# One transformer layer on one core: the MLP up projection by seven half-size products

## The reference

```
x = x + g1 * (mix_lat @ w_out)                       # attention part, before
h = modulate(x, g_mlp, sh2, sc2)                     # 1024 tokens x 1024
x = x + g2 * (square(relu(h @ w_mlp1)) @ w_mlp2)     # 1024 -> 4096 -> 1024
```

## Time and profile before

| what | value |
|---|---|
| runs | 1396.66, 1398.19, 1398.62 us |
| profiled execution: span, first to last instruction | 1394.5 us |
| profiled execution: its own time | not given apart from the span |
| mean granted TensorE clock | 0.994 |
| end of the last projection, start of the MLP's units | about 730 us |
| last stretch (down projection of chunk 7) starts | 1347.7 us |
| HBM read, written | 108.4 MB, 31.7 MB |

### The profile page before, as it was taken

One profiled execution on the slowest core, in us unless ns is written; L12 is line 12 of the kernel. 1 busy time (PEld: TensorE's weight loads), 2 busy tenths in 40 slices (PEclk: granted clock), 3 DMA queues, 4 the chain that ended last, 5 costly groups with the idle time before them and its releaser, 6 DMA issues.

```text
span 1394.5 us, 18825 instructions
## 1 busy us (share of the span) xinstructions
PE 1351.0 (97%) x7262; PEld 1144.5 (82%) x7262; DVE 914.7 (66%) x1284; ACT 692.6 (50%) x1343; POOL 487.0 (35%) x321
## 2 busy tenths in 40 slices
...
GB/s 376 189 172 161 173 159 290 125 90 86 128 197 141 183 131 192 71 1 61 37 71 121 32 30 91 31 76 31 69 40 27 91 31 76 31 64 44 15 61 121
DMA packets 121576, 143.42 MB, mean 103 GB/s; under 512 B 8184, under 2 KB 103288, under 8 KB 118672
## 3 DMA queue, kind: packets, MB, share of 16 engines
...
q0 software_dynamic: 256, 0.05, 0.0%
...
## 4 chain that ended last, share of the span: by engine, by line
PE 77%; DVE 12%; ACT 6%; DMA 2%; issue 1%; POOL 1%; SPq 0%; DVEq 0%; ACTq 0%
PE f_ps L2065 24%; PE f_ps L2334 19%; PE a_ps L1425 7%; PE o_ps L1773 6%; PE a_ps L1441 5%; PE a_ps L1471 5%; PE f_ps L2350 3%; ACT s_pr L1522 3%; DVE s_nmx L1607 2%; PE t_ps L956 2%; DMA t_wm<-in_w_mod 1%; PE t_ps L945 1%; PE t_ps L971 1%; ACT l_pr L1539 1%; DVE l_nb L1612 1%
## 5 line engine op out<-in xcount | busy, mean ns | idle before, releaser
L2065 PE MATMUL f_ps<-h,f_w 128*128 128x512 f32 x1536 | 358.0, 389 | 0.4 <-DVE h L1839 0.3
L2065 PEld LDWEIGHTS f_ps<-h,f_w 128*128 128x128 f32 x1536 | 288.2, 188 | 60.6 <-DVE h L1839 0.7
L2264 DVE TENSOR_TENSOR mix<-mix,f_ps 128x512 f32<-128x512 f32 x196 | 128.8, 684 | 152.8 <-PE f_ps L2334 152.8
L2105 POOL TENSOR_TENSOR f_w<-f_w,f_g 128x1024 f32<-128x1024 f32 x30 | 77.1, 2592 | 389.9 <-DMA f_w<-in_w_mlp 342.5
L2142 ACT ACTIVATE f_a<-f_ps 128x512 f32<-128x512 f32 x64 | 38.2, 597 | 255.0 <-PE f_ps L2065 254.9
L2334 PE MATMUL f_ps<-f_bl,f_ah 128*128 128x512 f32 x392 | 152.6, 389 | 0.0
L2334 PE MATMUL f_ps<-f_bh,f_ah 128*128 128x512 f32 x392 | 152.6, 389 | 0.0
L2334 PE MATMUL f_ps<-f_bh,f_al 128*128 128x512 f32 x392 | 152.5, 389 | 0.0
L1621 DVE TENSOR_TENSOR l_pT<-a_ps,l_pT 128x512 fp32r<-128x512 f32 (+1 forms) x192 | 109.0, 594 | 53.0 <-ACT l_pT L1532 53.0
L1425 PE MATMUL a_ps<-l_k,l_q 96*128 96x512 f32 (+1 forms) x576 | 136.4, 366 | 0.5 <-DVE l_mo L1633 0.5
L956 PE MATMUL t_ps<-w_in,t_h 128*128 128x416 f32 (+2 forms) x600 | 123.4, 351 | 0.3 <-DVE w_in L719 0.3
...
## 6 DMA issues: line engine op xcount, KB each, us to landing
...
f_w1r<-in_w_mlp SPq DMA_DIRECT2D x32, 512.0 KB, 4.1
f_w<-in_w_mlp SPq DMA_DIRECT2D x16, 1024.0 KB, 5.0
t_wm<-in_w_mod SPq DMA_DIRECT2D x8, 1024.0 KB, 12.6
...
```

The costliest lines, as they stand in the source:

```text
L2065: last = nc.tensor.matmul(ps[:, b, :], w1[:, g % 2, w, k, :], h2[x][:, k, half * HB:(half + 1) * HB], start=(k == 0 and i == 0), stop=(k = ...
L2264: V.tensor_tensor(x, x, ps[:, bank_of(i, t), :].rearrange("p (k c) -> p k c", c=P), ALU.add).then_inc(added, 1)
```

## The change

In chunks 1 to 7 the up projection is computed as seven half-size products P1 to P7. The token halves, the contraction halves and the column halves (256) of a chunk give 2 x 2 x 2 blocks; a product is 4 blocks of the contraction x 2 column tiles f x 3 = 24 matmuls, and there are seven instead of eight. A product's first operand is a block of h or one of four sums of them (s1 to s4, for P5, P6, P7 and P3), its second a quadrant of w1 or a difference. The sums don't depend on the chunk:
- In `out_phase` GpSimd sums `hn` (`sum_tile`) for tiles 4 to 7 and adds the parts of `h2` of the first half (`first_half`, 2048 elements a partition). `low_h` of tiles 4 to 7 waits for `sum_tile`.
- In chunk 0, which keeps its eight units in another order, GpSimd (`sum_parts`: three operations of 2048), VectorE (`fourth_sum`: two), ScalarE and VectorE (`sum_high`, `sum_low`: four each of 2048) make and split the four sums. SP stores them to DRAM, 2 MB each.
- In each later chunk SP streams them back in 16 pieces of 0.5 MB into a ring of six slots; four of these lie in room of `h2` that chunk 0 has finished with.
- w1 comes in quadrants of 0.5 MB. GpSimd makes four differences a chunk (`mix_quads`), ScalarE and VectorE split seven operands (`quad_high`, `quad_low`).
- In PSUM P3 adds to P5, and P6, P7, P4 add to P1 in turn. ScalarE copies P5, P3 and P2 out (six copies), VectorE adds P1, P6 and P7 to them (six additions); the results are then squared.
- The loads of w2 and its gates stand behind the new loads and differences in SP's and GpSimd's lists.
- Semaphores are reused from the first stage, some rooms are moved and a room X of 3072 words is added; the scratch for software DMA is set to 4096 bytes.

The core of the diff, where removed lines of the lists in the loops are left out:

```diff
+        for t in range(NB // 2, NB):
+            if t == NB - 1:
+                mlp.first_half()
+            mlp.sum_tile(t)
...
+            if t >= NB // 2:
+                dve.wait_ge(mlp.summed, mlp.summed_before + t + 1 - NB // 2)
...
-    ORDER = [(0, 0), (1, 0), (0, 1), (1, 1), (2, 0), (2, 1), (3, 0), (3, 1)]
+    ORDER = [(0, 0), (1, 0), (0, 1), (1, 1), (2, 1), (3, 1), (2, 0), (3, 0)]
+    P5, P3, P2, P1, P6, P7, P4 = range(7)
...
+    def load_quad(c, b):
+        if b == "12" and c > 1:
+            sp.wait_ge(w1_ready, split_no(c - 1, P7))
+        if b == "11":
+            sp.wait_ge(w1_ready, split_no(c - 1, P4) if c > 1 else FC)
+        if b == "22" and c > 1:
+            sp.wait_ge(w1_ready, split_no(c - 1, P4))
+        if b == "21":
+            sp.wait_ge(w1_ready, split_no(c, P3))
+            sp.wait_ge(quad_mixed, mixed_no(c, 2))
...
+    def load_piece(c, j, k):
+        n = piece(c, j, k)
+        if c == 1:
+            sp.wait_ge(s_stored[{P5: "s1", P3: "s4", P6: "s2", P7: "s3"}[j]], LOAD0 + 32)
+        if n >= RING:
+            before = n - RING
+            bc_, bj, bk = before // 16 + 1, (P5, P3, P6, P7)[before % 16 // 4], before % 4
+            if bk == 3:
+                sp.wait_ge(up_ready, unit(bc_, bj, 1))
+            else:
+                sp.wait_ge(piece_used, USED0 + 12 * (bc_ - 1) + 3 * STREAM[bj] + bk + 1)
+        elif n < HK:
+            sp.wait_ge(up_ready, 6)
+        else:
+            sp.wait_ge(s_stored["s3"], LOAD0 + 32)
+        sp.dma_start(quarter[n % RING].bitcast(F32), scr["hs"][STREAM[j], k].rearrange("i p n -> p i n")).then_inc(piece_loaded[n % RING], 16)
...
+    def sum_tile(t):
+        rows = slice(t * P, (t + 1) * P)
+        pool.wait_ge(o.scaled_h, 2 * t + 2)
+        G.tensor_tensor(sx[:, :, (t - NB // 2) * P:(t + 1 - NB // 2) * P], o.hn[:, 0:HK, rows], o.hn[:, HK:KC, rows],
+                        ALU.add).then_inc(summed, 1)
+    def first_half():
+        pool.wait_ge(o.y_ready, 2 * NB)
+        pool.wait_ge(o.h_ready, NB // 2)
+        G.tensor_tensor(s3[:, :, :], h2[0][:, 0:HK, 0:HB].bitcast(F32), h2[1][:, 0:HK, 0:HB].bitcast(F32), ALU.add).then_inc(s_made, 1)
+    def sum_parts():
+        pool.wait_ge(s_made, MADE0 + 1)
+        pool.wait_ge(summed, SUMMED0 + NB // 2)
+        G.tensor_tensor(s2[:, :, :], sx[:, :, :], s3[:, :, :], ALU.subtract).then_inc(s_made, 1)
+        pool.wait_ge(s_made, MADE0 + 2)
+        for i in range(2):
+            if i:
+                pool.wait_ge(s_made, MADE0 + 2 + i)
+            G.tensor_tensor(s3[:, :, :], s3[:, :, :], h2[i][:, 0:HK, HB:SEQ].bitcast(F32), ALU.subtract).then_inc(s_made, 1)
+    def fourth_sum(i):
+        if i == 0:
+            dve.wait_ge(s_made, MADE0 + 2)
+            V.tensor_tensor(s4[:, :, :], h2[0][:, HK:KC, 0:HB].bitcast(F32), s2[:, :, :], ALU.subtract).then_inc(s4_made, 1)
...
+    def sum_high(name):
+        if name == "s4":
+            act.wait_ge(s4_made, FOURTH0 + 2)
+            act.wait_ge(s_stored["s1"], LOAD0 + 32)
...
+    def sum_low(name):
+        dve.wait_ge(s_hi, SHI0 + SPLITS[name])
+        if name == "s1":
+            dve.wait_ge(s_made, MADE0 + 2)
+        V.tensor_tensor(lo[:, :, :], x[:, :, :], hi[:, :, :].bitcast(F32), ALU.subtract).then_inc(s_lo, 1)
...
+    def quad_high(c, j):
+        m = 7 * (c - 1) + j
+        act.wait_ge(up_ready, unit(1, m - 2, 1) if m >= 2 else UPS - 1 + m)
+        if j in (P3, P2, P1):
+            act.wait_ge(quad_loaded[{P3: "22", P2: "21", P1: "11"}[j]], LOAD0 + 16 * c)
+        else:
+            act.wait_ge(quad_mixed, mixed_no(c, {P5: 1, P6: 2, P7: 3, P4: 4}[j]))
...
+    def mix_quads(c, t):
+        if t == 1:
+            pool.wait_ge(quad_loaded["12"], LOAD0 + 16 * c)
+            pool.wait_ge(quad_loaded["11"], LOAD0 + 16 * c)
+        elif t == 2:
+            pool.wait_ge(quad_mixed, mixed_no(c, 1))
+            pool.wait_ge(quad_loaded["22"], LOAD0 + 16 * c)
+            pool.wait_ge(w1_ready, split_no(c, P5))
+        elif t == 3:
+            pool.wait_ge(quad_mixed, mixed_no(c, 2))
+            pool.wait_ge(w1_ready, split_no(c, P1))
+        else:
+            pool.wait_ge(quad_mixed, mixed_no(c, 3))
+            pool.wait_ge(quad_loaded["21"], LOAD0 + 16 * c)
+            pool.wait_ge(w1_ready, split_no(c, P6))
+        G.tensor_tensor(out, x, y, ALU.subtract).then_inc(quad_mixed, 1)
...
+        load_w1(2)
+        load_quad(1, "12")
+        load_quad(1, "22")
+        store_sum("s1", stage[0], sxl)
+        load_w1(3)
+        load_quad(1, "11")
+        store_sum("s2", stage[1], s2l)
+        store_sum("s4", stage[0], s4l)
+        store_sum("s3", sxh, s3l)
+        for k in range(HK):
+            load_piece(1, P5, k)
+        for k in range(2):
+            load_piece(1, P3, k)
         for c in range(1, NCH):
+            load_quad(c, "21")
+            for j, k in ((P3, 2), (P3, 3), (P6, 0), (P6, 1), (P6, 2), (P6, 3), (P7, 0), (P7, 1)):
+                load_piece(c, j, k)
+            if c < LAST:
+                load_quad(c + 1, "12")
+            load_piece(c, P7, 2)
+            load_piece(c, P7, 3)
+            if c < LAST:
+                load_piece(c + 1, P5, 0)
+                load_piece(c + 1, P5, 1)
+                load_quad(c + 1, "11")
+                load_quad(c + 1, "22")
+                for j, k in ((P5, 2), (P5, 3), (P3, 0), (P3, 1)):
+                    load_piece(c + 1, j, k)
             load_w2(c, 0)
             load_w2(c, 1)
...
+        pool.wait_ge(o.h_ready, NB)
+        sum_parts()
         pool.wait_ge(g2_loaded, 16)
-        pool.wait_ge(o.h_ready, NB)
         gate(0, 0)
+        mix_quads(1, 1)
         gate(0, 1)
         for c in range(1, NCH):
+            mix_quads(c, 2)
             mix_weights(c - 1)
+            mix_quads(c, 3)
+            mix_quads(c, 4)
+            if c < LAST:
+                mix_quads(c + 1, 1)
             gate(c, 0)
             if c < LAST:
                 gate(c, 1)
...
+            if n == 1:
+                sum_high("s1")
+            if n in (2, 3):
+                w1_high(n)
+            if n == 2:
+                sum_high("s2")
+            if n == 3:
+                sum_high("s4")
+                sum_high("s3")
+            if n == 6:
+                quad_high(1, P5)
         high(0, M1)
+        quad_high(1, P3)
         for c in range(1, NCH):
+            d = c - 1
+            high(d, M2)
+            copy(c, P5, 0)
+            copy(c, P5, 1)
+            quad_high(c, P2)
+            high(d, M6)
+            copy(c, P3, 0)
+            copy(c, P3, 1)
+            quad_high(c, P1)
+            copy(c, P2, 0)
+            high(d, M5)
+            high(d, M3)
+            copy(c, P2, 1)
+            quad_high(c, P6)
+            square(c, P1)
+            quad_high(c, P7)
+            quad_high(c, P4)
+            square(c, P6)
+            high(d, M7)
+            if c < LAST:
+                quad_high(c + 1, P5)
+            square(c, P7)
+            high(d, M4)
             if c < LAST:
                 high(c, M1)
+            square(c, P4)
+            if c < LAST:
+                quad_high(c + 1, P3)
...
+        sum_low("s1")
+        fourth_sum(0)
         w1_low(2)
+        fourth_sum(1)
+        sum_low("s2")
         w1_low(3)
+        sum_low("s4")
+        sum_low("s3")
+        quad_low(1, P5)
         low(0, M1)
+        quad_low(1, P3)
         for c in range(1, NCH):
             d = c - 1
             low(d, M2)
             row_sums(d)
             take(d, M1, 0, 1, 2, 3)
+            quad_low(c, P2)
             low(d, M6)
             take(d, M2, 0, 1)
+            quad_low(c, P1)
             take(d, M2, 2, 3)
             low(d, M5)
             take(d, M6, 0, 1, 2, 3)
             difference(d, M3)
             low(d, M3)
             take(d, M5, 0, 1)
+            quad_low(c, P6)
+            add(c, P1)
             take(d, M3, 0, 1)
+            quad_low(c, P7)
+            add(c, P6)
             take(d, M5, 2, 3)
+            quad_low(c, P4)
             difference(d, M7)
             low(d, M7)
+            add(c, P7)
             take(d, M3, 2, 3)
+            if c < LAST:
+                quad_low(c + 1, P5)
             low(d, M4)
             take(d, M7, 0, 1, 2, 3)
             if c < LAST:
                 low(c, M1)
                 take(d, M4, 0, 1, 2, 3)
+                quad_low(c + 1, P3)
...
+        def bank_free(c, j, f):
+            if j == P5:
+                pe.wait_ge(rect, 8 * (c - 1) + 6 + f + 1 if c > 1 else UPS)
+            elif j in (P3, P2, P1):
+                pe.wait_ge(up_copied, copied_no(c, {P3: P5, P2: P3, P1: P2}[j], f))
+            else:
+                pe.wait_ge(up_added, added_no(c, {P6: P1, P7: P6, P4: P7}[j], f))
...
+        def up_streamed(c, j):
+            pe.wait_ge(w1_ready, split_no(c, j))
+            for k in range(HK):
+                n = piece(c, j, k)
```

(50 more changed lines are left out.)

181 lines of the change are left out of this document (114 added, 67 removed).

## The result

The changed kernel takes 1405.38 us (median of four runs, 1404.05 to 1406.35). The kernel before, beside it on the same chip, took 1397.99. The ratio is 1.0052 [1.0037, 1.0066]: slower by 7.4 us, though TensorE has 168 matmuls fewer to do.

A forecast was written before the change was run, and what follows sets the result against it. TensorE was taken to bound the kernel: -38.1 (matmuls) + 24.6 (P5's later start) + 1.5 (clock) + 17.7 (chunk heads) = +5.7 on 1398.2, so 1403.9 us; range 1380 to 1416, its own case 1391 to 1411.

The forecast's parts named there:

- The matmuls removed: Chunks 1 to 7: seven products of 24 matmuls stand for eight, 38.1 us less TensorE.
- The port: VectorE operations with two SBUF inputs and GpSimd ones exclude each other whole, alternate, and GpSimd goes first at a tie.
- The stores: Before P5 of chunk 1: 6.8 MB of stores take 18.2 us, first piece 3.6; P5 24.6 us later, chunk 0 included.
- "5.6 us" for tile 7: Before chunk 0's up units: `first_half` delays tile 7's split from 743.5 to 749.1, 5.6 us.
- The clock in P5: P5 after the idle stretch runs at the lower clock level: 1.5 us, bounds 0 and 3.
- The head of the chunk: Crowded GpSimd and VectorE work leaves TensorE idle 2.95 us in each of chunks 2 to 7: 17.7 us.
- M2's third tile stalls with it until 24.7: Head of chunks 2 to 7: M6's low parts delay M2's take, so this tile stalls until 24.7 instead of 21.8.
- The base: Profiled span 1394.5 us, median 1398.2; the 3.7 us between them taken to lie around the span.
- The range: Own range 1391 to 1411: clock 0 to 3, stores 16 to 24, 1.2 to 3.9 us a chunk.
- 2 (VectorE gets between long operations): Chunk 0: VectorE gets in during long GpSimd operations, so nothing waits; P5 6 us late, 1366 us; chance 0.13.
- 3: Chunk head: w2's first gate pushes M4's low part back, M2 stalls by 4 to 5 us; 1418 us; chance 0.12.
- 1 (the head holds): Chunk head: gates end before 0, row sums in time, only chunk 0 costs; 1386.2 us; chance 0.27.

The follow-up runs named there:

- e10_first_half_late: Changed kernel with GpSimd's `first_half` moved from ahead of tile 7's sum to behind the last split of h: 1410.4 us.
- e5_w2_early: Changed kernel with w2's first half loaded right behind quadrant 11, ahead of quadrant 22 and four pieces: 1410.44 us.
- e9_w2_both_early: Changed kernel with both w2 halves loaded before quadrant 22, M4 split earlier, chunk 0's w1 splits earlier and first gates later: 1385.77 us, 0.9905 to before.
- e11_p5_first: The e9_w2_both_early kernel with the four loads of P5's pieces of chunk 1 issued ahead of the stores of s4 and s3: 1387.67 us.

## Where the prediction was right and where it was off

The sign, the size (1403.9 for 1405.4) and both places were right; the terms fared as follows.

- **The matmuls removed**: 168 fewer (7262 and 7094), 38.1 us at the 5.44 us of 24.
- **The port**: instructions exclude each other whole, alternate, and GpSimd wins the tie at 755.3. Tile 7's split ended at 750.54 (predicted 749.1, and this execution was 1.75 late by then), `w1_low(2)` at 771.87 (771.3), `w1_low(3)` at 779.59 (779.2).
- **The stores**: from there to P5 22.1 us (21.8). The stores alone took 20 us, 6.8 MB at 341 GB/s, for 18.2 taken; the first piece followed 1.7 us behind them instead of 3.6. (The estimate of 19.0 us from the figure of about 358 GB/s in DMA: Bandwidth & Descriptors, section Bandwidth, of the Trainium skill was nearer; the window shows 355 for stores, though 400 where loads run.) The whole term was 24.6 for 23.4 measured.
- **"5.6 us" for tile 7** was counted as if on the path. e10_first_half_late shows that it isn't by itself: with it gone, P5 started where it had. What counts is the length of GpSimd's and VectorE's chain through the sums, and `first_half` is part of that wherever it stands. By this reading the number survived because either way the chain is longer by one operation.
- **The clock in P5**: 1.5 was taken, 2.6 measured. This term of the sum was mis-sized. The same fall inside chunk 0 was left out: behind its two gaps the units ran at 0.79 (744 to 755) and 0.76 (772 to 780), and four of them took 24.33 us for 21.8. That cost nothing, since the path led through the sums.
- **The head of the chunk**: 17.7 predicted, 18.25 measured, but made up otherwise. The step "M2's third tile stalls with it until 24.7" failed: TensorE stalls once, before P2, by some 2.15 us a chunk (12.9 / 6), and waits for M2's take 0.2 us in all. Of the other 0.9 us, 0.75 are lost behind that stall: P2's 12 matmuls take 3.0 to 4.5 us instead of 2.72, and the ones after them a little more too. The walk also had w2's first half land at -10; it landed at -7.5, though the loads ahead of it had been named.
- **The base**: "3.7 us longer, which I take to lie around the span" was wrong. Some 1.85 us lie around it; the rest was that one execution's lead on the median. The forecast of the difference stands apart from this: 5.7, for 7.4 between the medians and 6.6 between the traces without the 1.75.
- **The range**: the three bounds, taken all at one end, give 1389.7 and 1416.9, wider than the "own range" of 1391 to 1411. The result lies inside either.
- **Rivals.** 2 (VectorE gets between long operations) is excluded by the 5.52 us split. 3 didn't occur in the change, and e5_w2_early brings it about in small. 1 (the head holds) didn't occur either, but its condition was named rightly: once the gates end before zero (e9_w2_both_early) the chunk is 76.60, and the kernel takes 1385.8 where rival 1 said 1386.2. That agreement is partly luck: this kernel has also 2.1 us less in chunk 0 and still 0.4 more in each later one.

What stays open: the 10 us before P5 in the best version, or the 11.6 before M1 in e11_p5_first. They lie behind the stores, and making the sums earlier, or storing less, wasn't tried. What makes the clock fall in one chunk and not in the next is open too.
